# Attention and mLSTM products in half-array tiles, with turned attention output and mLSTM values inside the last projection

## The reference, cut to what matters

```python
s_own = jnp.einsum('bhqd,bhkd->bhqk', qc, k_own) * scale
s_own = jnp.where(own_pos[None, :] <= q_pos[:, None], s_own, -jnp.inf)
p_own = jax.nn.softmax(s_own, axis=-1)
return jnp.einsum('bhqk,bhkd->bhqd', p_own, v_own)
```

## Time and profile before

| | us |
|---|---|
| median of three runs | 1054.43 (1053.37 to 1055.22) |
| the profiled execution | 1053.28 |
| its span | 1051.5 |
| PE busy in the span | 1029.2 (98%) |
| DVE busy | 505.6 (48%) |
| ACT busy | 408.7 (39%) |

### The profile page before, as it was taken

The page is one execution under the profiler, slowest core; times in us unless marked ns, Lnnn a source line. Parts: engine busy times, 40 slices in busy tenths (PEclk is TensorE's granted clock), DMA queues, the critical chain, the costliest instruction groups (busy, mean ns, idle before and its releaser), DMA issues.

```text
span 1051.5 us, 13819 instructions
## 1 busy us (share of the span) xinstructions
PE 1029.2 (98%) x5650; PEld 693.0 (66%) x5650; DVE 505.6 (48%) x714; ACT 408.7 (39%) x645; POOL 22.2 (2%) x42
## 2 busy tenths in 40 slices
PE   9999999999999999999999999999999999999886
PEld 6888878888999999898897544444444444444332
DVE  5676677987987754766665412111212111211112
ACT  7634634436444444664744222222222222222112
POOL 1000000010000000100000000000000000000000
PEclk9999999999999999899999999999999999999998
DMA  9977548976888753474355999999999999999993
GB/s 330 391 272 249 191 160 287 321 252 231 291 315 296 250 185 136 124 269 158 107 201 215 372 415 422 420 421 421 419 421 421 420 422 420 420 423 420 420 421 141
DMA packets 86179, 327.89 MB, mean 312 GB/s; under 512 B 5744, under 2 KB 5904, under 8 KB 61408
## 3 DMA queue, kind: packets, MB, share of 16 engines
q1 hardware_dynamic: 84768, 323.45, 79.7%
q0 software_dynamic: 1344, 3.50, 1.0%
HBM read 325.88 MB, written 1.05 MB: 311 GB/s over the span
## 4 chain that ended last, share of the span: by engine, by line
PE 48%; DMA 8%; DVE 1%; ACT 1%; issue 0%; ACTq 0%
PE bank L1024 18%; PE bank L1047 8%; DMA raw<-in_w_expert_up 3%; DMA es<-in_w_expert_up 3%; PE bank L1066 3%; PE bank L992 3%; DMA e_wlo<-in_w_expert_up 3%; PE bank L579 2%; PE bank L582 2%; PE bank L585 2%; PE bank L1033 1%; PE bank L549 1%; PE bank L555 1%; PE bank L552 1%; PE bank L1006 1%; PE bank L1008 1%
## 5 line engine op out<-in xcount | busy, mean ns | idle before, releaser
L1613 DVE TENSOR_TENSOR wlo<-raw,whi 128x2048 fp32r<-128x2048 f32 x87 | 199.1, 2289 | 95.4 <-ACT whi L1121 95.0
L1121 ACT ACTIVATE whi<-raw 128x2048 fp32r<-128x2048 f32 x87 | 165.9, 1912 | 97.3 <-PE bank L555 38.2
L2236 DVE SCALAR_TENSOR_TENSOR YS<-bank,wsl,gate2q 128x512 f32<-128x512 f32 x32 | 24.0, 751 | 217.0 <-PE bank L1047 217.0
L1024 PE MATMUL bank<-es,XT 128*64 128x512 f32 x336 | 117.4, 604 | 5.1 <-DMA es<-in_w_expert_up 3.8
L1024 PE MATMUL bank<-raw,XT 128*64 128x512 f32 x352 | 119.8, 597 | 0.0
L552 PE MATMUL bank<-wlo,hh 128*128 128x512 f32 x224 | 87.6, 391 | 1.6 <-DVE wlo L1613 1.4
L549 PE MATMUL bank<-whi,hh 128*128 128x512 f32 x224 | 88.0, 393 | 0.6 <-ACT whi L1128 0.6
L555 PE MATMUL bank<-whi,hl 128*128 128x512 f32 x224 | 87.3, 390 | 0.0
L1024 PEld LDWEIGHTS bank<-es,XT 128*64 128x64 f32 x336 | 35.1, 139 | 77.3 <-issue 76.4
L1024 PE MATMUL bank<-e_whi,XT 128*64 128x512 f32 x168 | 76.1, 595 | 2.4 <-DMA e_wlo<-in_w_expert_up 2.4
L1024 PE MATMUL bank<-e_wlo,XT 128*64 128x512 f32 x168 | 76.2, 596 | 0.0
(11 more groups left out here) (386 smaller groups left out, 1940.1 us busy)
## 6 DMA issues: line engine op xcount, KB each, us to landing
raw<-in_w_in SPq DMA_DIRECT2D x41, 1024.0 KB, 6.4
raw<-in_w_expert_up SPq DMA_DIRECT2D x33, 1024.0 KB, 22.0
raw<-in_w_ff SPq DMA_DIRECT2D x32, 1024.0 KB, 5.4
es<-in_w_expert_gate SPq DMA_DIRECT2D x32, 1024.0 KB, 22.4
raw<-in_w_ada SPq DMA_DIRECT2D x24, 1024.0 KB, 5.9
raw<-in_w_expert_down SPq DMA_DIRECT2D x22, 1024.0 KB, 26.0
e_whi<-in_w_expert_gate SPq DMA_DIRECT2D x21, 1024.0 KB, 23.4
e_wlo<-in_w_expert_up SPq DMA_DIRECT2D x21, 1024.0 KB, 25.5
```

The costliest lines, as they stand in the source:

```text
L1024: m = e.matmul(b[64 * w:64 * w + 64, :], K.XT[j // 4 % 2][:, k, j % 4, :], K.weights(halves[w])[:, 512 * c:512 * c + 512], start=k == 0, s ...
L1121: e.activation(whi[n % RING][:, :], raw[h.raw][:, :], ACT.Copy).then_inc(S["hi"], 1)
L1613: e.tensor_tensor(wlo[n % RING][:, :], raw[h.raw][:, :], whi[n % RING][:, :].bitcast(F32), ALU.subtract).then_inc(S["lo"], 1)
```

## The change

It does the following.

- The scores of an even and an odd head alternate, so that two consecutive matmuls use different row halves of the array.
- The attention probabilities are divided by their sums on DVE before they are transposed (four `tensor_tensor`), and the transposes fill three banks of 512 columns for each half in place of four of 384. ACT copies one bank of the three, DVE two.
- The attention values are the stationary operand (64 columns, two heads side by side in column halves), and the probabilities are streamed. The result is already turned: the transposes `mxT2`, `mxT3` and DVE's scaling of the output are gone, and `mix_hi`, `mix_lo` read `av0`, `av1`.
- The mLSTM values carry a 129th column of ones for each head, so the sum comes with the product. The first token half is computed in the middle of OM, the second right behind OM. DVE's division runs in two instructions for each token half in place of four, and ACT's squares are moved ahead of the attention's `mix_hi`.
- The router's shift is multiplied and summed over chunks on DVE (`wrp`, `wrq`), and PE adds it up in one matmul.
- Both `turn_h` stand before piece 87, and `lo(89)` stands before `head_lo(0)`.
- Banks are dealt out anew.

All eight squares now stand ahead of `mxh`, four of them ahead of the gate's copy. The core of the diff:

```diff
-            use(f"pt0{hq}", ((0, 1, 5, 6)[hq], "pt_a" if hq % 2 else "pt_d", hq // 2 + 1))
-        use("OM", (2, "omt", 1), (3, "omt", 2))
...
+        use("OM", (0, "omt", 1), (1, "omt", 2))
+        use("pt0", (2, "pt_d", 1), (3, "pt_a", 1), (5, "pt_d", 2))
+        use("ml0", (6, "mnum", 1), (7, "mnum", 2))
+        use("pt1", (4, "pt_d", 3), (2, "pt_a", 2), (3, "pt_d", 4))
+        use("ml1", (5, "mnum", 3), (4, "mnum", 4))
+        use("av0", (2, "x_lo", SPLIT["mx"] + 1))
+        use("av1", (3, "x_lo", SPLIT["mx"] + 2))
...
+    for hq in range(4):
+        for t in range(2):
+            for half in range(2):
+                b0, b1, b2 = K.at[f"att{half}"]
+                p = slice(64 * half, 64 * half + 64)
+                q0, k0 = K.qaT[p, hq, :], K.qaT[p, 4 + hq, :]
...
+    def mlstm_values(t):
+        free(f"ml{t}")
...
+        for h in range(4):
+            o = K.at[f"ml{t}"][h // 2][:, 129 * (h % 2):129 * (h % 2) + 129]
+            for s_ in range(t + 1):
+                m = e.matmul(o, K.ET[:, h, s_, 128 * t:128 * t + 128], K.vmt[:, s_, h, :], start=s_ == 0, stop=s_ == t)
+        m.then_inc(S["out_mm"], 1)
+
+    def middle_om():
+        att_turn(0)
+        mlstm_values(0)
         att_turn(1)
...
-            e.matmul(b[:, 64 * hq:64 * hq + 64], P[:, hq, 0:128], vv[0], start=True, stop=True)
-            e.matmul(o1, P[:, hq, 128:256], vv[0], start=True, stop=False)
-            m = e.matmul(o1, P[:, hq, 256:384], vv[1], start=False, stop=True)
...
+                    m = e.matmul(b[64 * half:64 * half + 64, o + 128 * s_:o + 256], K.vat[s_][:, 64 * h:64 * h + 64],
+                                 K.PTt[half][:, hq, 256 * s_:256 + 128 * s_], start=s_ == 0, stop=s_ == 1,
+                                 skip_group_check=True)
...
+    e.wait_ge(S["wrp"], 2)
+    e.matmul(K.at["shift"][0][:, 0:36], C("ones"), K.wrq[:, :], start=True, stop=True).then_inc(S["shift_mm"], 1)
...
         if g:
             turn_h(0)
+            turn_h(1)
         free(f"wo2_{g}")
         dense_half(86 + g, K.mxh, K.mxl, 1, K.at[f"wo2_{g}"], True, False, (lambda k: SPLIT["mx"] + k // 2 - 1))
-    turn_h(1)
...
+            e.tensor_tensor(Sx[:, :, o], Sx[:, :, o],
+                            stat(k + 16 + 4 * t, 4).unsqueeze(2).broadcast_to([128, 4, o.stop - o.start]),
+                            ALU.mult).then_inc(S["att"], 1)
...
     probs_turned(0)
     lo(86)
     probs_turned(1)
-    e.wait_ge(S["shift_mm"], 1)
...
+    heads(0)
...
+    e.tensor_tensor(K.wrp[:, :, :], K.wr[:, :, :], K.ada_cols[:, 16:24].unsqueeze(2).broadcast_to([128, 8, 36]),
+                    ALU.mult).then_inc(S["wrp"], 1)
+    e.wait_ge(S["wrp"], 1)
+    e.tensor_reduce(K.wrq[:, :], K.wrp[:, :, :].rearrange("p c n -> p n c"), AX, ALU.add).then_inc(S["wrp"], 1)
     lo(87)
...
+    heads(1)
+    lo(88)
...
-    head_lo(0)
     lo(89)
+    head_lo(0)
     head_lo(1)
```

More of the change, by code:

```diff
@@ L468, in place_psum @@
         use("x3T01", (1, "h2T_a", 2))
[L469 removed]
+        use("x3T10", (0, "h2T_a", 3))
         use("x3T11", (6, "h2T_d", 1))
         use("warm", (3, "h2T_a", 1))
[L472 removed]
+        use("rank", (1, "rt", 22))
         for k in range(4):
@@ L807, in pe_program @@
     dense("VA", 80, K.nh, K.nl)
[L810 to L823, removed]
+    free("att0")
+    free("att1")
+    e.wait_ge(S["qaT"], 4)
+    for hq in range(4):
[4 more added lines that the diff above has]
+                q0, k0 = K.qaT[p, hq, :], K.qaT[p, 4 + hq, :]
+                if t == 0:
+                    e.matmul(b0[:, 128 * hq:128 * hq + 128], q0[:, 0:128], k0[:, 0:128], start=True, stop=True)
+                else:
+                    m = e.matmul((b1, b2)[hq // 2][:, 256 * (hq % 2):256 * (hq % 2) + 256], q0[:, 128:256], k0,
+                                 start=True, stop=True)
+                    if hq == 3:
+                        m.then_inc(S["mix_mm"], 1)
     def mlstm_scores():
@@ L836, in att_turn @@
     def att_turn(half):
[L837 to L847, removed]
-        att_turn(1)
[L849 to L868, removed]
-            e.matmul(b[:, 64 * hq:64 * hq + 64], P[:, hq, 0:128], vv[0], start=True, stop=True)
-            e.matmul(o1, P[:, hq, 128:256], vv[0], start=True, stop=False)
-            m = e.matmul(o1, P[:, hq, 256:384], vv[1], start=False, stop=True)
+        e.wait_ge(S["att"], 2 * half + 2)
@@ new lines, in att_turn @@
+        free(f"pt{half}")
+        for i in range(12):
+            hq, j = divmod(i, 3)
+            m = e.transpose(K.at[f"pt{half}"][i // 4][:, 128 * (i % 4):128 * (i % 4) + 128],
+                            K.SX[half][:, hq, 128 * j:128 * j + 128], C("ident"))
+            if i % 4 == 3:
+                m.then_inc(S["pt_mm"], 1)
+    def mlstm_values(t):
+        free(f"ml{t}")
+        e.wait_ge(S["sc"], 8)
+        e.wait_ge(S["vmt"], 2)
+        e.wait_ge(S["gw_z"], 3)
+        for h in range(4):
[3 more added lines that the diff above has]
+        m.then_inc(S["out_mm"], 1)
@@ new lines, in middle_om, with att_values @@
+    def middle_om():
+        att_turn(0)
+        mlstm_values(0)
+        att_turn(1)
+    dense("OM", 84, K.nh, K.nl, mid=middle_om)
+    mlstm_values(1)
+    def att_values(n):
+        free(f"av{n}")
+        b = K.at[f"av{n}"][0]
+        for hq in (2 * n, 2 * n + 1):
+            o = 256 * (hq % 2)
+            for s_ in range(2):
+                for half in range(2):
+                    h = 2 * hq + half
+                    m = e.matmul(b[64 * half:64 * half + 64, o + 128 * s_:o + 256], K.vat[s_][:, 64 * h:64 * h + 64],
+                                 K.PTt[half][:, hq, 256 * s_:256 + 128 * s_], start=s_ == 0, stop=s_ == 1,
+                                 skip_group_check=True)
@@ L872, in att_values @@
         m.then_inc(S["out_mm"], 1)
+    e.wait_ge(S["pt_d"], 4)
+    e.wait_ge(S["pt_a"], 2)
+    e.wait_ge(S["vat"], 2)
     att_values(0)
     att_values(1)
[L876 to L892, removed]
+    free("shift")
@@ L1401, in act_program @@
     hi(83)
-    leave("VA", 40, K.vat, 0, ACT.Copy, "vat", False)
+    e.wait_ge(S["used"], 82)
+    for t in range(2):
+        e.activation(K.vat[t][:, :], K.at["VA"][t][:, :], ACT.Copy).then_inc(S["vat"], 1)
     hi(84)
@@ L2362, in pool_program @@
     e.wait_ge(S["used"], 72)
+    e.memset(K.vmt[:, :, :, 128:129], 1.0).then_inc(S["gw_z"], 1)
     e.dma_start(K.ghb[:, :], A["g_mlstm_head_2"].broadcast_to([128, 512])).then_inc(S["l_late"], 16)
```

152 lines of the change are left out of this document (79 added, 73 removed).

## The result

The changed kernel takes **1047.3 us**, the median of eight runs (1044.6 to 1051.3), against 1054.0 of before (1053.4 to 1055.2, eight runs): a ratio of 0.994 with a 95% interval from 0.9923 to 0.9957. Forecast were 1048.0 us and a range of 1046.0 to 1051.2. The profiled execution took 1046.66 us, its span is 1044.9 where that of before is 1051.5. All times here are of undisturbed executions; only the last kernel of the experiments had others, two of six (1148.7 and 2073.7 us), and they are left out.

The account below looks back on a forecast made before the run. PE's arrival at the experts starts the transfer stream and so sets the end. PE loses 8.5 us of work, 2.1 become a new wait, 6.4 are gained: 1053.28 to 1046.9, as a median 1048.0 us, range 1046.0 to 1051.2.

Parts of the forecast that it names:

- scores: Sixteen attention score products on PE: row halves run together, 4.89 us become 2.9, saving 2.0 (ends 0 and 2.45).
- values: Attention value products on PE: column halves run together, 5.30 us become 2.8 with switches, saving 2.5 (ends 0 and 2.7).
- piece 86: PE products behind the new wait, ahead of piece 87 and `last`: 5.5 us, plus about 0.25 of stall.
- load 18: First expert load needing a used-up buffer, released by PE's first expert pieces: from 594.44 us to near 588.
- The frame: Whole second half: PE's arrival at the experts starts the transfer stream, so moving it moves the end by as much.
- The new wait: PE ahead of piece 86, ended by ACT's `mxh`: 2.1 us of the 8.5 us saved turn into waiting.
- T: Moment PE enters the middle of OM, forecast at 524.5 us; later steps are counted from it.
- mLSTM values: On PE, 24 one-column products go and 12 wide ones stay: about 3.7 us in place of 5.3, saving 1.6.
- rival A: PE's clock halves behind the new wait: piece 86, perhaps 87, lose 1.6 to 3.2 us; 1049.6 to 1051.2; chance 0.24.
- the chain behind T: ACT and DVE steps from OM's middle on: piece 86 starts 17.0 us after T, `last` 29.5 us after.
- Rival B: Scores and values: array halves don't run together at so few columns; gain 4.1 us, 1050.3; chance 0.10.
- Rival D: PE from piece 86 on: half clock stays through some 22 us of products, costing 22 us more, 1070; chance 0.03.

Follow-up runs that it names:

- the last kernel of the experiments: Changed kernel with ACT's evictions before the second squares, constant products before the last three experts, `lo(88)` behind and `brb` ahead of the normalisation; 1043.6 to 1045.9 us, ratio 0.9922.
- held load: Changed kernel with expert load 7 held back until PE has finished the first quarter of `last`; 1047.7 us, ratio 0.9941.
- held PE: Changed kernel with four constant matmuls, 3.5 us on PE, just ahead of the first expert; 1050.1 us, ratio 0.996.
- the order by halves: Changed kernel with all eight attention value products of the even heads, of both banks, ahead of the eight of the odd heads; its one execution took 1049.2 us.
- single scores: Changed kernel with the scores in the old order, all even heads ahead of the odd ones; 1050.0 us, ratio 0.9965.
- reordered values: Changed kernel with attention values ordered even, even, odd, odd within each pair of heads; 1047.8 us, ratio 0.9948.
- products ahead of the last experts: Changed kernel with constant identity products on PE ahead of the weight waits of experts 29, 30 and 31; 1046.5 us, ratio 0.9934.

## Why the prediction was right

Step by step, in the changed kernel's profile:

| | forecast | measured |
|---|---|---|
| scores | 2.9 | 2.82 |
| PE enters the middle of OM | 524.5 | 524.65 |
| values | 2.8 | 2.75 |
| piece 86 starts | 541.5 | 541.22 |
| the wait ahead of it | 2.1 | 2.54 |
| piece 86, with the stall at its start | 5.75 | 6.98 |
| `last` starts | 554.0 | 554.54 |
| load 18 | 588 | 588.46 |
| gain in the profiled execution | 6.4 | 6.6 |

**The frame** was right: PE starts the stream of transfers, so that its arrival at the experts is what counts. The held load and the held PE show both halves of this; the low DMA share ahead of load 18 alone had only suggested it.

**The scores** were sized rightly and shown to reach the experts: 2.0 us less in the kernel before, and piece 86 2.0 us later in the changed one without them.

**The new wait** stood where forecast and was ended by what was forecast, ACT's `mxh`. With 8.5 us of work gone, PE is ahead of ACT. So the values' saving, correct as a size (2.55 against 2.5), is worth nothing by itself, as the order by halves shows: 2.0 us more of values, no change at the experts. The wait was 0.4 longer than forecast: PE was free 14.0 us behind T in place of 14.9, ACT's eviction 0.4 earlier too. Most of that is the mLSTM values, the term that was sized worst: 12 wide products at 0.30 us were to take 3.7 us, and they took 0.89 in the middle of OM and 1.88 behind it, 2.8. No run has the mLSTM values, the router's shift or the missing transposes alone, so what each is worth is read from rows only.

**Two terms were off and cancelled, and that is luck.** The forecast left the clock at full behind the wait; in this profile it stood at half until 544.3, which cost 1.2 (82.08 against 80.86). That is rival A, at the low end of its price or below: piece 86 took 1.1 to 1.65 us longer than the 5.75 at full clock, where 1.6 to 3.2 were priced. It was given a chance of 0.24 and happened in five of the seven profiles with a wait of 2.5 us ahead of piece 86, and in none of the five with a wait of 0.3 to 0.8 there. The text had also named a half clock behind the wait as a sign of being wrong; it came, and the time still lay in the range, which reached over rival A. The other way, the chain behind T was priced 0.8 too long: piece 86 starts 541.22 - 524.65 = 16.6 behind T in place of 17.0, and its end and the two transposes were put 1.15 us apart, with the bank free 22.9 behind T. DVE was done with it at 546.73, 22.1 behind T, and the transposes take 0.8. The rest is 0.2 us up to T and 0.1 behind `last`. At full clock the whole way is 80.87 us, a gain of 88.37 - 80.87 = 7.5 where 6.4 was forecast; behind the half clock it is 6.3.

**Rival B** is refuted for rows and columns alike (4.89 and 4.75 us in single file against 2.82 and 2.75). **Rival D** didn't occur: in all five profiles the clock was back at full before piece 86 ended.

**What the text didn't foresee** is the spread. Half clock at expert 31 cost 2.8 us in one profile and 1.6 in another; a later transfer and a longer stretch behind PE's last products cost 0.9 to 1.6 each. Which of these makes the runs above 1050 us long stays open, since only one of the five was profiled.

## What to carry to other kernels

When work is taken out of the engine that bounds a stretch, ask at once which engine is late next, and read its queue for instructions that nobody waits for ahead of the one that somebody does: here four squares stood ahead of the eviction. A waiting matmul waits for its inputs and for its bank, and the bank's last reader can be a tiny instruction at the end of another queue; look it up before moving anything ahead of it. A pairing in half the array pays only as far as the wait behind it doesn't swallow it, so price the pair and the wait together.

## What the runs showed of the hardware

- Products in half tiles run in pairs even at 128 and 256 moving columns: 16 score products in 2.82 us in place of 4.89, 16 value products in 2.75 in place of 4.75. The value products needn't alternate one by one; two and two did as well (2.8), eight and eight did not.
- A wait of the same length brings half clock in one execution and not in another. Ahead of piece 86 it followed in five profiles: the changed kernel, its repetition, single scores, reordered values and the held load (waits of 2.49 to 2.55). It fell at different moments: by 541.0, still in the wait, in the changed kernel, and 1.2 us after PE had begun again with single scores. It didn't follow in these two:

```profile
541.31 0.47 PE L548 MATMUL bank<-whi,mxh 128*128 128x512 f32 x1 [2.54 <-ACT mxh L1457]
```

```profile
541.57 0.47 PE L548 MATMUL bank<-whi,mxh 128*128 128x512 f32 x1 [2.54 <-ACT mxh L1457]
```

The first is the kernel with products ahead of the last experts, the second that with PE held up; neither is edited ahead of this row. Waits of 0.3 to 0.8 us there never brought it (five profiles). In the expert loop it followed behind waits of 1.95, 2.21, 2.85 (twice), 2.87 and 3.37 us, and didn't behind 2.02, 2.07, 2.40, 2.71 and 3.11. The longest that left the clock at full, with single scores:

```profile
985.99 0.61 PE L1020 MATMUL bank<-e_whi,XT 128*64 128x512 f32 x1 [3.11 <-DMA e_wlo<-in_w_expert_up]
```

And the 2.21, in the kernel with the values reordered, some 1 us after the work had begun again:

```profile
983.49 0.61 PE L1020 MATMUL bank<-e_whi,XT 128*64 128x512 f32 x1 [2.21 <-DMA e_wlo<-in_w_expert_up]
...
984.41 1.06 PE L1020 MATMUL bank<-e_whi,XT 128*64 128x512 f32 x1
```

So the length of the wait alone doesn't decide.
